# A hybrid mixer kernel on Trainium2: the gated delta stage for both directions at once, and the head norm inside the output projection

## The reference

```python
def chunk_gated_delta(q, k, v, g, beta, s0):
    ...
    gcum = jnp.cumsum(g, axis=-1)
    decay = jnp.exp(jnp.where(incl, gcum[..., :, None] - gcum[..., None, :], -jnp.inf))
    kb = k * beta[..., None]
    lower = jnp.where(strict, jnp.einsum('bhnid,bhnjd->bhnij', kb, k) * decay, 0.0)
    tinv = lax.linalg.triangular_solve(eye + lower, jnp.broadcast_to(eye, lower.shape),
                                       left_side=True, lower=True, unit_diagonal=True)
    u = tinv @ (v * beta[..., None])
    w = tinv @ (kb * jnp.exp(gcum)[..., None])
    attn = jnp.where(incl, jnp.einsum('bhnid,bhnjd->bhnij', q, k) * decay, 0.0)
    ...
    def step(S, inp):
        qd, kd, ui, wi, ai, gl = inp
        v_new = ui - wi @ S
        o = qd @ S + ai @ v_new
        S = S * gl[..., None, None] + jnp.einsum('bhcd,bhce->bhde', kd, v_new)
        return S, o
...
# bidirectional_gated_delta: d = 0 forward, d = 1 on flipped tokens; context first, its state starts the latent part; outputs summed
# gated_rms_norm: y = rms_norm_2(o, w) * silu(gate), per head, then concatenated with attention and multiplied by w_out
```

## Time and profile before

| | us |
|---|---|
| median of 3 runs (3699.72 to 3703.4) | 3702.68 |
| the profiled execution | 3707.26 |
| its span in the profile | 3705.5 |
| gated delta stage, d = 0: make, chunks | 149, 45 |
| gated delta stage, d = 1: make, chunks | 142, 47 |
| head norm and wait for the projection | 22 |

### The profile page before, as it was taken

How to read it: one execution, slowest core, us unless ns; L and a number is a source line. 1 busy time by engine, 2 the same in 40 slices (tenths; PEclk the granted TensorE clock), 3 DMA queues, 4 the chain that set the end, 5 groups by cost and what they waited for, 6 DMA issues and landing times. The chain is left out here.

```text
span 3705.5 us, 44179 instructions
## 1 busy us (share of the span) xinstructions
PE 3394.9 (92%) x18732; PEld 1866.4 (50%) x18732; DVE 1217.6 (33%) x2054; ACT 586.7 (16%) x1078; POOL 683.0 (18%) x432
## 2 busy tenths in 40 slices
PE   8998999999999889889999999999778877799998
PEld 3454444744444578533444443647577763444432
DVE  1443043013022466412444015423656461301112
ACT  1023030001000433100000011102532320100001
POOL 0000011000000444101996810001631210000000
PEclk9989999998999899999999999899999898899999
DMA  4211223210231000132343521222100003599996
GB/s 154 73 35 40 79 69 102 74 63 12 74 108 46 2 3 4 61 116 85 120 136 123 163 82 41 80 63 75 52 1 1 1 1 129 218 409 409 409 409 263
DMA packets 120514, 406.24 MB, mean 110 GB/s; under 512 B 13824, under 2 KB 18560, under 8 KB 120064
## 3 DMA queue, kind: packets, MB, share of 16 engines
q1 hardware_dynamic: 113408, 378.25, 28.9%
q0 software_dynamic: 6912, 25.17, 2.1%
HBM read 399.17 MB, written 4.19 MB: 109 GB/s over the span
## 5 line engine op out<-in xcount | busy, mean ns | idle before, releaser
L422 PE MATMUL ps<-arena 128*128 128x512 f32 (+1 forms) x3952 | 1696.9, 591 | 70.6 <-DVE arena L565 17.2
L422 PEld LDWEIGHTS ps<-arena 128*128 128x128 f32 x3952 | 756.5, 193 | 1008.6 <-issue 979.5
L2629 PE MATMUL ps<-arena 128*64 128x512 f32 x1024 | 238.7, 600 | 5.0 <-PE ps L2659 2.6
L1488 POOL TENSOR_TENSOR arena<-arena 128x512 f32<-128x512 f32 x64 | 80.2, 1270 | 752.2 <-DVE arena L1590 658.8
L2220 PE MATMUL ps<-arena 128*128 128x128 f32 x1312 | 174.1, 294 | 24.1 <-POOL arena L2275 21.1
L473 DVE SCALAR_TENSOR_TENSOR arena<-ps,params,arena 128x511 f32<-128x511 f32 (+4 forms) x266 | 190.6, 717 | 9.4
L2776 POOL TENSOR_SCALAR arena<-arena,small 128x1024 f32<-128x1024 f32 x64 | 183.7, 2870 | 7.9 <-DMA arena<-in_w_mod 3.9
L2220 PEld LDWEIGHTS ps<-arena 128*128 128x128 f32 x1312 | 167.0, 206 | 28.9 <-issue 15.4
L467 DVE TENSOR_SCALAR arena<-ps,params 128x512 f32<-128x512 f32 x68 | 55.0, 809 | 374.4 <-PE ps L422 374.4
L1855 POOL TENSOR_SCALAR arena<-arena,small 128x768 f32<-128x768 f32 x32 | 70.1, 2203 | 441.5 <-DVE small L1835 441.5
L453 ACT ACTIVATE arena<-arena 128x512 f32<-128x512 f32 (+2 forms) x60 | 36.1, 601 | 693.0 <-DVEq L477 693.0
(11 more groups left out here) (408 smaller groups left out, 3292.4 us busy)
## 6 DMA issues: line engine op xcount, KB each, us to landing
arena<-in_w_in SPq DMA_DIRECT2D x166, 512.0 KB, 3.6
arena<-in_w_gate SPq DMA_DIRECT2D x128, 512.0 KB, 11.5
arena<-in_w_up SPq DMA_DIRECT2D x128, 512.0 KB, 15.0
arena<-in_w_down SPq DMA_DIRECT2D x128, 512.0 KB, 9.4
arena<-in_w_mod POOLq DMA_DIRECT2D x48, 512.0 KB, 4.2
arena<-in_ffn_up SPq DMA_DIRECT2D x44, 512.0 KB, 3.6
arena<-in_w_branch SPq DMA_DIRECT2D x32, 512.0 KB, 3.6
arena<-in_w_out SPq DMA_DIRECT2D x16, 512.0 KB, 3.7
```

Source lines behind the costliest of these rows:

```text
L422: last = nc.tensor.matmul(out[0:m, 0:j["n"]], w[:, q * m:(q + 1) * m], j["rhs"](ka + q), start=(ka + q == 0), stop=(ka + q == kt - 1))
L1488: tt = lambda o, x, y, op: nc.gpsimd.tensor_tensor(o, x, y, op)
L2629: ins = nc.tensor.matmul(k.bank(b + f)[64 * e:64 * e + 64, :], XE(p)[:, q * P + 64 * e:q * P + 64 * e + 64], slot(g + e)[:, f * 512:f * 51 ...
```

## The change

The four phases become one, `gdn_phase`, for both directions.

- Six groups g of 16 chunks: 2 tiles of 4 heads of one direction; even g forward, odd g backward, the first two context. All products of the solve are quarter products (`cells`: 8 cells of 64 columns, two halves, 16 products of 64x64 a step). A step covers 16 chunks and fills one bank.
- In each level Y = LM X, X = X - XT Y, XT = XT - Y XT: X is no longer a turned XT. DVE subtracts, ACT copies Y. The masks are 64 columns wide.
- The decay matrix is exp(-|difference|), one Abs and one Exp on ACT, in place of max, min and two Exp; beta and the other factors are applied to the inverse (XV, XK) rather than to keys and values. KD is multiplied in place on POOL.
- The plan has 10 blocks of 16 beats. In block b: PREPARE of group b (R, KK, LT, QK, X0), levels 1 to 4 of group b - 1 (12 steps `A`, in two banks), SOLVE of group b - 2 (Y5, kt0, XT5, kt1, vt0, vt1, U0, U1, W, E0, E1, in banks 2, 3 and 7 in turn), and in blocks 4, 6 and 8 the chunks of a pair of groups, one chunk of each direction every four beats: `chunk_u`, then the result of the chunk before, then `chunk_state`. QK, E0, E1 and results are for latent groups alone.
- POOL makes masks, diagonals and state times decay (SG); DVE adds the product to it.
- The head norm is the `ahead` of the output projection (`HeadNorm`). In all tiles the products on the attention half (q = 4 to 7) now come first, and before q = 0 of the first tile stand the four spreads.
- Constants of 128 columns a mask go, those of 64 columns come: 1536 columns less in sum. The arena has 90 planes for 87.

```diff
-                        for q in range(kn):
+                        for n in range(kn):
+                            q = (n + 4) % 8 if isinstance(ahead, HeadNorm) else n
                             if ahead is not None and i == 0:
-                                pe.wait_ge(*ahead.ready_at(ka + q))
+                                if q == 0 and isinstance(ahead, HeadNorm):
+                                    ahead.pe_spread(pe)
+                                if ahead.ready_at(ka + q)[1]:
+                                    pe.wait_ge(*ahead.ready_at(ka + q))
...
+class HeadNorm:
...
+    def ready_at(self, c):
+        return self.ready, min(c, 3) + 1 if c < 4 else 0
...
+    def pe_spread(self, pe):
+        k = self.k
+        pe.wait_ge(self.root, 1)
+        for c in range(4):
+            if c >= 2:
+                pe.wait_ge(self.used, c - 1)
+            k.nc.tensor.matmul(k.bank(6 + c % 2), k.const("sel")[0:4, c * P:(c + 1) * P], self.rows, start=True, stop=True).then_inc(self.spread, 1)
...
-def gdn_make_phase(k, d, qs, ks, vs, cp, keep, own):
+def gdn_phase(k, q, kv, ctx_kv, cp, y, planes, late):
...
+    A = [f"{s}{n}" for n in (1, 2, 3, 4) for s in ("Y", "X", "XT")]
+    BLOCKS = GROUPS + 4
+    BEATS = 16
+    PREPARE = {0: ["R"], 4: ["KK"], 7: ["LT"], 9: ["QK"], 12: ["X0"]}
+    SOLVE = {0: ["Y5"], 1: ["kt0"], 2: ["XT5"], 3: ["kt1"], 4: ["vt0"], 5: ["vt1"], 7: ["U0"], 8: ["U1"], 10: ["W"], 12: ["E0"], 14: ["E1"]}
+    ON_DVE = ("R", "KK", "QK", "XT5", "E0", "E1")
...
+            def cells(b, l, r):
+                for t in range(8):
+                    for z in range(2):
+                        other = ident[rows(z), rows(z)] if r is None else r[rows(z), cell(t)]
+                        ins = nc.tensor.matmul(k.bank(b)[rows(z), cell(t)], l[rows(z), cell(t)], other, start=True, stop=True)
+                return ins
...
+                elif s == "W":
...
+                    for t in range(8):
+                        for z in range(2):
+                            ins = nc.tensor.matmul(k.bank(banks_of[s, g][z])[:, cell(t)], KD(g, t // 4)[rows(z), wide(t % 4)], XK[rows(z), cell(t)],
+                                                   start=True, stop=True)
...
+            for b in range(BLOCKS):
+                for beat in range(BEATS):
+                    u, n = chunk(b, beat), beat // 4
+                    if u is not None:
+                        if beat % 4 == 0:
+                            chunk_u(u, n)
+                        elif beat % 4 == 1 and u >= 1 and n >= 1:
+                            chunk_result(u, n - 1)
+                        elif beat % 4 == 2:
+                            chunk_state(u, n)
...
+                    for s, g in steps(b, beat):
+                        step_m(s, g)
+                    if 1 <= b < GROUPS + 1:
+                        for s in a_steps(beat):
+                            step_a(s, b - 1)
...
+                    if 1 <= b < GROUPS + 1:
+                        if beat == 0:
+                            level_mask(b - 1, 1)
+                        for s in a_steps(beat):
+                            if s[0] == "Y":
+                                level_mask(b - 1, int(s[1]) + 1)
+                    if 2 <= b < GROUPS + 2:
...
+                        if lat(g) and beat in (9, 13):
+                            ti = (beat - 9) // 4
+                            if ti == 1:
+                                pool.wait_ge(m_made, made_at("E0", g))
...
+                            tt(heads(DIAGE), ident.unsqueeze(1).broadcast_to([P, 4, P]), by_head(C_EGC, g, ti)).then_inc(diage_ok, 1)
+                        if beat == 11:
+                            pool.wait_ge(m_made, made_at("W", g))
```

More of the change, by code:

```diff
@@ new lines, in gdn_phase @@
+    pl = k.pl
+    GROUPS = 6
+    direction = lambda g: g % 2
+    lat = lambda g: g >= 2
+    first_tile = lambda g: 0 if g < 2 else 2 * ((g // 2 - 1 + direction(g)) % 2)
+    at = iter(planes)
+    take = lambda n: [pl(next(at)) for _ in range(n)]
+    A_SET = [take(5) for _ in range(2)]
+    LT, LM, X, XT, Y = (lambda g, n=n: A_SET[g % 2][n] for n in range(5))
+    F, MB, DIAG, DIAGE, VT0, VT1, XV, XK = take(8)
+    S_, SG_, VN_ = take(4), take(2), take(2)
+    VT = (VT0, VT1)
+    S = lambda n, d: S_[2 * (n % 2) + d]
@@ new lines, in gdn_phase @@
+    ORDER = [step for b in range(BLOCKS) for beat in range(BEATS) for step in steps(b, beat)]
+    BANKS = (2, 3, 7)
+    banks_of, users, turn, last_user = {}, {}, 0, {}
+    for step in ORDER:
+        n = 2 if step[0] == "W" else 1
+        banks_of[step] = [BANKS[(turn + i) % 3] for i in range(n)]
+        turn += n
+        users[step] = [last_user[b] for b in banks_of[step] if b in last_user]
+        for b in banks_of[step]:
+            last_user[b] = step
+    m_made, m_act, m_dve = (k.sem(f"g_m_{x}") for x in ("made", "act", "dve"))
@@ new lines, in _ @@
+            for b in range(BLOCKS):
+                for beat in range(BEATS):
+                    u, n = chunk(b, beat), beat // 4
+                    if u == 1 and beat % 4 == 1 and n >= 1:
+                        result(1, n - 1)
+                    if b == 7 and beat == 1:
+                        result(1, 3)
+                    for s, g in steps(b, beat):
+                        step_m(s, g)
+                    if b < GROUPS and beat == 1:
+                        factors(b)
+                    if 1 <= b < GROUPS + 1:
+                        for s in a_steps(beat):
+                            if s[0] == "Y":
+                                g = b - 1
+                                act.wait_ge(a_made, a_made_at(s, g))
+                                if s == "Y1" and g >= 2:
+                                    act.wait_ge(m_made, made_at("XT5", g - 2))
+                                nc.scalar.activation(Y(g), k.bank(A.index(s) % 2), ACT.Copy).then_inc(a_act, 1)
@@ L2262, in _ @@
         @block.gpsimd
         def _(pool):
[L2264 to L2275 removed]
+            tt = lambda o, x, z, op=ALU.mult: nc.gpsimd.tensor_tensor(o, x, z, op)
@@ new lines, in _ @@
+            for d in range(2):
+                nc.vector.memset(S(0, d), 0.0).then_inc(st_ok, 1)
+            for b in range(BLOCKS):
+                for beat in range(BEATS):
+                    u, n = chunk(b, beat), beat // 4
+                    if u is not None:
+                        if beat % 4 == 0:
+                            chunk_new(u, n)
+                        elif beat % 4 == 1 and u == 2 and n >= 1:
+                            result(2, n - 1)
+                        elif beat % 4 == 2:
+                            chunk_next(u, n)
+                    elif b == 9 and beat == 1:
+                        result(2, 3)
+                    for s, g in steps(b, beat):
+                        step_m(s, g)
+                    if 2 <= b < GROUPS + 2 and beat == 3:
+                        scaled(b - 2)
+                    if b < GROUPS and beat == 10:
+                        start(b)
+                    if 1 <= b < GROUPS + 1:
+                        for s in a_steps(beat):
+                            step_a(s, b - 1)
```

702 lines of the change are left out of this document (395 added, 307 removed).

## The result

The changed kernel takes 3576.39 us, the median of 4 runs (3571.3 to 3584.19), against 3702.3 us before (3699.72 to 3703.4). The ratio is 0.9663, 95% interval 0.9642 to 0.9684: 126 us faster. The forecast was 3560 us, with 3540 to 3605 as its range. The time lies in the range and is 16 us above the forecast.

The account below looks back on a forecast made before the run. The kernel was taken as a chain of TensorE stages, TensorE busy 92%. The stage falls from 382 to 251 us (206 work, 45 waits), 131 less; with the norm's 11.5, 142.5 off the median 3702.68: 3560 us, range 3540 to 3605.

Parts of the forecast that it names:

- TensorE's work: New delta stage: TensorE's products, turns and shape changes sum to 206 us, against 308 us busy before.
- The quarter step: New stage: 16 pairs of 64x64 records cost 0.95 us and treat 16 chunks; 106 such steps, 100.7 us.
- the 0.15 us for a change: New stage: each change of product shape on TensorE costs 0.15 us; 123 changes, 18.4 us.
- rival 1: The 106 quarter steps: products don't pair, a step takes 2.5 us, +163 us, 3723 us, slower; 3%.
- the 2.3 us a step: Quarter steps: the step time from which rival 1 decides, 142.5/106 above 0.95; over 1.5 us would show the prediction wrong.
- The waits: New stage, walked through ten blocks: TensorE waits 48 us, less 3 counted twice with shape changes, so 45 us.
- Rival 2: Five full blocks: each of 16 beats exposes a 0.6 us handover, +48 us, 3608 us; 13%.
- The tail: Blocks 8 and 9, the chain of the last four chunk pairs: 28 us with 19 of products, 9 waiting.
- the old chunks parts: Old delta stage, second part of each direction's pass: 45 and 47 us, TensorE back to back, clock 0.99.
- The make parts: Old delta stage, first part of each direction's pass: 149 and 142 us, TensorE busy 113 and 108, clock 0.87.
- The head norm: Norm inside the output projection: weights come beside it, one product behind the last ready head; 11.5 us less.
- Rival 3: Head norm not shortened: first products run at 1.2 GHz and spreads hold the second half; 11.5 us stay, 3572 us; 8%.

Follow-up runs that it names:

- halves_apart: Changed kernel with each quarter step's products reordered, all eight of rows 0 to 63 first, then all eight of rows 64 to 127; 3677.78 us.
- no_fill: Changed kernel with split_result's order, GpSimd's diagonals ahead of the level masks and a second diagonal buffer for the last E1, no unread products; 3548.16 us.
- the two exchanges: Changed kernel with the old head norm as its own phase, 3585.57 us; kernel before with only the norm moved into the projection, 3690.2 us.
- the second profile: Profiled execution of the changed kernel run once more, unedited, in a later set; median 3573.33 us, the traced execution 3578.28 us.
- warm_tail: Changed kernel with thirteen unread 512-column products added in TensorE's waits of block 8; 3566.58 us.
- split_result: Changed kernel with, in blocks 8 and 9, results in own banks and cut in two, VN products behind the state product, output sums later; 3569.04 us.

## Why the prediction was right, and where it was short

**TensorE's work** was forecast at 206 us. Blocks 0 to 7 have 195.2 us of it in the trace, where the sum had 187 (206 less the tail's 19); blocks 0 and 1 are at a clock of 0.62 and 0.90. The quarter step of 0.95 us is 0.93 between equal shapes and 1.08 where the shape changes, so the step and the 0.15 us for a change are both borne out by these rows. Two slips of the working are too small to matter: 12 x 8 x 0.11 is 10.6 and not 10.8, and the waits add up to 48.5 and not 48.

**The pairing** (rival 1) was given 3% on the row of line 1239, against the Trainium skill's "TensorEngine Tiling (Array Packing)", Gotcha 1, by which different row tiles can't access one PSUM bank at the same time. The trace agrees with the row and not with the page: both halves of a cell go into one bank, and halves_apart shows that their order is worth 101 to 104 us, 55 to 72 of them by the steps at 2.4 GHz and the rest by the clock that fell with it. The price of the rival was too high, though. An unpaired record starts about 0.05 us after the last (4.91 us less 0.22, by 96), not 0.077 as in line 1363. The 2.3 us a step from which the rival would decide aren't reached at 2.4 GHz (1.90). At 1.2 GHz they are: a step of halves_apart takes 3.31 us there, so the rival had a second price that the prediction did not look at.

**The waits** were forecast at 45 us and are 31.3 (261.5 us less 230.2 busy). Busy time taken from the length of each window, they are 7.1 us in block 0 (forecast 11), 2.8 in block 1 (4.5), 1.7, 1.7 and 1.2 in blocks 2 to 4 (3 each), 3.4 in block 5 (3.5), 1.2 in block 6 (2.5), 3.0 in block 7 (4) and 9.0 in the tail (9). So the walk from queue to queue gave each of them to within 4 us, and in the middle it was pessimistic throughout, by handovers that overlap. E1 does wait for GpSimd, four times, 7.0 us. Rival 2, that each beat pays its handover, is wrong: it needed some 10 us a block. Block 3 was put at 28 us and is 27.2.

**The tail** is the step that failed: "28 us with 19 of products, so 9 waiting". The waits were right, 9.0 us. The 19 us are right at 2.4 GHz only, where no_fill has 19.2; in the changed kernel the same products keep TensorE busy for 35.1 us. The durations were those of the old chunks parts, whose clock was 0.99 and 1.00, and I took them over without asking which clock a chain with 2 us of waits in each chunk would have. The term is 44.1 us, 16 more. The make parts and the norm, with their 0.87 and 0.68, were the rows to ask.

**The head norm**: -11.5 forecast, -6.4 in the first profile, 10.1 and 10.3 to 13.7 by the traces of the two exchanges. The weights do come beside the norm, and the attention half runs in its shade (8 records in 3.70 us behind the sums). The 19.1 us from square to first tile are 24.1 and 21.0 in two profiles, 20.4 behind the old stage and 19.9 at best. Two steps of that term were off. "The chain up to 3064.8 is the same" is not: the spreads start 11.7 us after the first square in the kernel after, 9.1 before, since the sums take 6.23 us instead of 3.60. And "behind the last ready head there is only one product" is not what the code does. All four spreads stand ahead of q = 0 in TensorE's order, so the four products on the delta half follow one another behind the last spread:

```profile
2947.24 9.34 PE L422 MATMUL ps<-arena 128*128 128x512 f32 x15
2948.08 0.75 DVE L626 SCALAR_TENSOR_TENSOR arena<-arena,params 128x512 f32<-128x512 f32 x1
...
2953.61 0.75 DVE L494 SCALAR_TENSOR_TENSOR arena<-ps,mods,arena 128x512 f32<-128x512 f32 x1 [4.79 <-PE ps L422]
```

The last head is ready at 2948.83, the first tile is taken 4.8 us later instead of 1.2 (2.9 in the second profile). An order with each spread ahead of its own product was not run. Rival 3 named the right kind of cause. It had the first products and the spreads at 1.2 GHz; the first products ran at 2.4, and the sums were slow, and of the spreads those of the first profile (6.11 us, 4.35 in the second). It took the loss as all or nothing; about half of its 11.5 us came in the one profile, and less in the other.

**The sum** of the profile is 120.8 + 6.4 = 127.2 us instead of 142.5. Of the 15.3 us between, the tail made 16 and the norm 5, and blocks 0 to 7 gave 6 back: their waits are 22 us instead of 36, their work 195 instead of 187. So the total came as near as it did partly by luck, through errors of opposite sign.

**What was named beforehand**: a stage of 245 to 260 us is 261.5 and 258.9; TensorE above 80% busy is 88% (230.2 of 261.5 us); a clock near 1.0 after the first 20 us holds for blocks 2 to 7 (0.95 to 1.00), and for the tail it doesn't. That last point was the one to watch.

## What to carry to other kernels

Price a product by its shape and by the neighbour that it follows: the same 16 products cost 1.15 or 1.90 us by the order of their row halves alone. Where a stage ends in a serial chain, price its rows at both clock levels, and look at the last wait ahead of the chain rather than at the chain: here a wait of 2.2 us stood ahead of a tail that took 44 us instead of 28, and in the execution of no_fill that was traced, without it and with the results in split_result's order, the tail ran at full clock and took 24. Don't count on a high clock being handed over a wait to what follows: warm_tail's tail ended at 2.4 GHz, and the sums behind its next wait, 1.78 us, took 6.48 us instead of 3.60. And let a projection's phase begin ahead of the norm that feeds it, so that its weights come beside the norm.

## What the runs showed of the hardware that I had not expected

TensorE can be busy without a gap and stay at 1.2 GHz. In split_result it had no wait from 2883 us to the end of the stage at 2914 us, and a clock of 0.50; in no_fill the same products, entered at 2.4 GHz, kept that clock through waits of 0.94 and 1.39 us. In halves_apart it was busy 50.0 of 50 us at 0.71, low from about 2898 to 2928 us, and then at 2.4 GHz again with the same kinds of products as before. Behind a wait of the same 2.33 us the changed kernel was low for less than 5 us in one profile (2823.2 to 2827.7) and not at all in the other. What was tried and helped was to remove the last idle stretch ahead (together with GpSimd's order), or a few 512-column products (in warm_tail the first u product behind six records of them takes 1.09 us again). Which activity decides is not shown by these runs.
